# A block of attention, pooling and 64 experts on one core: a small expert group second, the p product in the routing stage, the shared expert once and late

## The chip, the core and the metric

The kernel runs on one core of a Trainium2 chip. Its time is the device time in microseconds, median of the runs. A core has five engines with a queue of instructions each: PE (matrix products, with weight loads beside them), DVE (vectors), ACT (scalar functions, also a cheap way out of PSUM), POOL (which here issues the gathers and scatters of rows) and SP (which issues most other transfers). Sixteen DMA engines move the data. The engines wait for each other by semaphores.

## The reference

One layer on x of 512 tokens by 1024, all in float32:

```
h = rmsnorm(x)
x = x + (sigmoid(g_a) * pool_branch(h) + sigmoid(g_b) * attention_branch(h)) @ w_out
h2 = rmsnorm(x)
scores = sigmoid(h2 @ w_router)                    # 64 experts, 8 chosen for each token
x = x + swiglu(h2, shared expert) + sum over the chosen experts of weight * swiglu(h2, expert)
x = x + sigmoid(rmsnorm(x) @ w_ple_gate) * rmsnorm(p @ w_ple_proj, g_ple_post)
```

An expert has three matrices of 1 MB: gate and up (1024 x 256 each) and down (256 x 1024). The shared expert has the same shapes and works on every token. p is 512 x 256, w_ple_proj 256 x 1024 (1 MB).

## The kernel before

Each engine has its program, written out by hand in the order of time; nothing is scheduled by a planner.

**Start.** PE first multiplies a tile of zeros with itself (`WARMING` times, L1796), then transposes the first 128 rows of x (`strided_T`, L1785) and takes the first half of Q (`first_q`, L1809) with weights called q0. SP loads x, q0, q1 and so on in the order of use.

**Dense part**, to about 320 us: Q, K, V, pooling, gates, attention, the two branches, `out_proj` (L2026), the second norm and the router.

**Routing**, about 320 to 341 us. DVE picks 8 experts for each token, ranks the tokens of every expert, and sorts the experts by a key: experts 0 to 3 first, the others by their count. `perm` is the matrix that turns a rank into a place in this order. While PE waits for these steps it takes products that nobody waits for yet: in the kernel before, the gate and up products of the shared expert for the first two of the four tiles of 128 tokens (`shared_up`, L2097, eight products of 512 columns for a tile). The rows of h2 go to DRAM (`h_rows`), and POOL gathers from there the rows of each expert step (`gather`, L812) as soon as the list of the step is made.

**Expert stage**, about 341 to 904 us. The 64 experts in sorted order make 16 groups of four. A large group has 96 places for each expert, so 384 rows, three steps of 128; a small group has 64, so two steps (`cap_of`, `steps_of`). Before, groups 0 to 7 are large and 8 to 15 small: 40 steps. A step r on PE is `up(r)` (L2273, 64 products of 32 rows), transposes of the step before, `rows_T(r + 1)`, the lists of a later group (`lists`), late jobs, and `down(r - 1)` (L2302). The weights of four experts fit into the ring of twelve 1 MB slots (`EXPERT_SLOT`: slots 9, 0, 3, 6 and the two behind each; gate, up, down). SP refills a slot when PE has done with it: `load_in` waits for `gu_ps`, `load_down` for `y_ps`, all in one fixed order (`load_group`). The ring is full with the first four experts when the stage begins, apart from what the code loads late.

**Late jobs** are small pieces that PE does between the parts of a step, at the steps listed in `JOB_STEP`: the shared expert for the last two tiles (`late_T`, `late_up`, L2072, L2083, L2086), its transposes, its down product (`shared_down`, L2222, then `base` on DVE), and the product p x w_ple_proj (`ple_proj`, L2233, then `ple_square` on ACT and `ple_gain` on DVE). `SMALL_AT` is 24, the first step of group 8. The weights of the shared expert are loaded twice: into the ring for the first two tiles, and into other buffers for the last two.

**Tail**, from about 904 us: the scattered results are summed, the last norm, w_ple_gate and the output.

Of the kernel before, what the change touches and what calls it, by code (L numbers as in the profile page):

```python
# [14 lines left out]
P = 128  # L15
# [25 lines left out]
WARMING = 14  # L41
# [8 lines left out]
BIG_GROUPS = 8  # L50
CAP2 = 64
LESS = CAP - CAP2
STEP_OF = [(g, s) for g in range(NGROUP) for s in range(GROUP * (CAP if g < BIG_GROUPS else CAP2) // P)]
STEPS = len(STEP_OF)
FIRST_STEP = [STEP_OF.index((g, 0)) for g in range(NGROUP)]
TCOL, WCOL = 2, 4
LCOL = TCOL + 2 * WCOL
LATE = (2, 3)
SMALL_AT = GROUP * CAP * BIG_GROUPS // P
JOB_STEP = [SMALL_AT + n // 2 for n in range(8)] + [SMALL_AT + 6 + n // 2 for n in range(4 * NT)]  # L60
# [13 lines left out]
C_ALL = C_IC + NG * PAD  # L74
# [7 lines left out]
def cap_of(g):  # L82

    return CAP if g < BIG_GROUPS else CAP2
# [19 lines left out]
def constant_table():  # L104
# [14 lines left out]
    for g, at in ((0, C_PAIR), (BIG_GROUPS, C_PAIR2)):  # L119
        for step in range(steps_of(g)):  # L120
            for k in range(STRIPS):
                second = strip_expert(g, step, k) - pair_of(g, step)
                c[k * STRIP:(k + 1) * STRIP, at + 2 * step + second] = 1
    for g, w in enumerate(POOL_WINDOWS):
        c[:, C_IC + g * PAD:C_IC + (g + 1) * PAD] = 1.0 / np.minimum(np.arange(PAD) + 1, w)
# [8 lines left out]
def alibi_table():  # L134
# [18 lines left out]
    ["wa0", "wa1", "wb0", "wb1"] + [f"out{c}" for c in range(4)] + ["shg", "shu"]  # L153
DENSE_SLOT = [u % 8 for u in range(13)] + [8, 9, 10, 11] + [1, 2, 3, 4, 6, 7]
# [5 lines left out]
SH_BANK = [7, 3, 5, 5]  # L160
# [21 lines left out]
def build(nc, t, y_dram, h2_dram, out):  # L182
    ctx = ExitStack()
    with ctx:
# [49 lines left out]
        sh_row = hi[:, 0:NT * FE].rearrange("p (i f) -> p i f", i=NT)  # L234
        sh_act = hi[:, 2 * T:4 * T].rearrange("p (j n) -> p j n", j=2)
        w_shd = hi[:, 2 * D:4 * D].rearrange("p (j n) -> p j n", j=2)
# [4 lines left out]
        shg_late = hi[:, 2 * D:4 * D].rearrange("p (k n) -> p k n", k=KD)  # L241
        shu_late = [w.rearrange("p (k n) -> p k n", k=KD // 2) for w in (lo3, hi[:, D:2 * D])]
# [7 lines left out]
        pT = qa[:, 0:1024].rearrange("p (j n) -> p j n", j=2)  # L250
        r_sc, r_sel, r_w, r_rank = (qa[:, 1024 + k * NR:1024 + (k + 1) * NR] for k in range(4))
# [25 lines left out]
        w_ple = [rows[:, 3, :], flat_actT[:, 3 * D:4 * D]]  # L277
# [17 lines left out]
        def bank(b, n=1):  # L295
# [26 lines left out]
        mid_loaded, late_loaded, sh_late_loaded = sem("mid_loaded"), sem("late_loaded"), sem("sh_late_loaded")  # L322
# [5 lines left out]
            sem("ple_ps"), sem("ple_squared"), sem("ple_copied"), sem("ple_rstd"))  # L328
        logit_ps, scores_ready = sem("logit_ps"), sem("scores_ready")
# [34 lines left out]
        def unit_source(name):  # L364
# [13 lines left out]
            if name == "shg":  # L378
                return t["w_sh_gate"][0].rearrange("(k p) n -> p k n", p=P)
            if name == "shu":  # L380
                return t["w_sh_up"][0].rearrange("(k p) n -> p k n", p=P)
# [101 lines left out]
        def _(sp):  # L483

            released_by = {"q0": (qkv_ps, 2 * NT), "q1": (qkv_ps, 2 * NT), "kv": (qkv_ps, 2 * NT)}
            released_by |= {"pool0": (gate_ps, 14), "pool1": (gate_ps, 14)}
# [31 lines left out]
            for u in range(8, DENSE_AT["shg"]):  # L518
                load_dense(u)
# [4 lines left out]
            for u in range(DENSE_AT["shg"], N_DENSE):  # L524
                load_dense(u)
# [37 lines left out]

            load_in(0, 0)
            load_down(0, 0)
            load_part(1, 1, 0)
            load_down(2, 2)
            load_down(3, 3)
# [4 lines left out]
            load_in(2, 2)  # L573
            sp.wait_ge(logit_ps, NT)
            sp.wait_ge(pT_ps, 2)
            sp.wait_ge(sel_ready, NT)
            sp.wait_ge(gathered[0], 16)
            sp.dma_start(shg_late, unit_source("shg")).then_inc(sh_late_loaded, 16)
            for c in range(2):
                sp.dma_start(shu_late[c], unit_source("shu")[:, 4 * c:4 * c + 4, :]).then_inc(sh_late_loaded, 16)  # L580
            sp.dma_start(gpost, t["g_ple_post"].broadcast_to([P, D])).then_inc(late_loaded, 16)
            sp.wait_ge(shared_ps, 2)
            load_in(3, 3)
            sp.wait_ge(order_ready, 1)

            def load_ple_proj():
                sp.wait_ge(tokw_ready, 1)
                for j in range(2):
                    sp.dma_start(w_ple[j], t["w_ple_proj"][0][j * P:(j + 1) * P, :]).then_inc(late_loaded, 16)

            def load_shared_down():
                sp.wait_ge(shared_ps, NT)
                sp.dma_start(w_shd, t["w_sh_down"][0].rearrange("(j p) n -> p j n", p=P)).then_inc(late_loaded, 16)

            def load_group(g, late):
# [6 lines left out]
                if e:  # L602
                    in_used(step)
                    load_in(pos, e[0])
                    if g == 1:
                        load_ple_proj()
                    if g - 1 >= BIG_GROUPS:
# [5 lines left out]
                if e and g - 1 < BIG_GROUPS:  # L613
# [9 lines left out]
                elif e:  # L623
                    in_used(step + 1)
                    if step == SMALL_AT + 2:
# [263 lines left out]
        def _(act):  # L889
# [86 lines left out]
            second_rows(3)  # L976
            act.wait_ge(maskedT_ps, 1)
# [3 lines left out]
            def shared_silu_of(i):  # L981
                act.wait_ge(shared_ps, i + 1)
                nc.scalar.activation(sh_row[:, i, :], bank(SH_BANK[i])[:, 0:FE], ACT.Silu,
# [9 lines left out]
            def silu(r, k):  # L993
                act.wait_ge(gu_ps, STRIPS * (r + 1))
                nc.scalar.activation(esilu[k], bank(2 + k)[:, 0:FE], ACT.Silu).then_inc(silu_ready, 1)  # L995
# [1464 lines left out]
```

## Time and profile before

| | us |
|---|---|
| median of 3 runs | 985.17 (983.69 to 985.89) |
| profiled execution | 985.45 |
| its span, first to last instruction | 983.6 |
| PE busy | 937.1 |
| DVE, ACT, POOL busy | 361.7, 162.7, 226.5 |
| chain of work that ended last | PE 74%, DMA 21% of the span |

The span is what the trace covers; the 1.8 us between it and the time of the execution lie outside. A busy PE may still be behind its peak, and idle time on another engine costs nothing by itself. The chain of work goes back from the last instruction to what released it, step by step.

### The profile page before, as it was taken

How to read it: one execution, taken by the hardware profiler on the slowest of the kernel's cores; microseconds unless marked ns; L12 is line 12 of the kernel's file. 1: busy time of each engine (PE TensorE's matmuls, PEld its weight loads, DVE VectorE, ACT ScalarE, POOL GpSimd, SP SyncE). 2: the span in 40 equal slices, each digit the busy share in tenths (PEclk: the TensorE clock that was granted, in tenths of full speed). 3: DMA queues.
4: the chain of work that ended last, by engine and by line, in shares of the span. 5: the costliest groups of instructions: out<-in, count | busy, mean ns of one | idle time of the engine just before them, and what ended most of it. 6: DMA issues, size and time to landing. Idle time of an engine off the chain costs nothing.

```text
span 983.6 us, 15761 instructions
## 1 busy us (share of the span) xinstructions
PE 937.1 (95%) x6411; PEld 492.3 (50%) x6411; DVE 361.7 (37%) x776; ACT 162.7 (17%) x304; POOL 226.5 (23%) x344
## 2 busy tenths in 40 slices
PE   9999999999999999999999999999889899897798
PEld 8688888888556533333333333344323233332344
DVE  3765674336436733333332110111101111111687
ACT  2001234210011211111111111111101112121021
POOL 4216923262000212222222222212111211201110
PEclk9999999999999999999999999999989999999899
DMA  9940006322472799999999999999999999999972
GB/s 335 329 128 1 1 1 208 135 86 79 142 304 107 242 383 395 395 418 400 404 421 411 402 417 409 411 420 422 415 421 422 421 419 416 421 398 372 368 274 86
DMA packets 83913, 301.06 MB, mean 306 GB/s; under 512 B 9299, under 2 KB 35959, under 8 KB 59648
## 3 DMA queue, kind: packets, MB, share of 16 engines
q1 hardware_dynamic: 70144, 263.19, 68.0%
q0 software_dynamic: 11920, 33.63, 8.8%
q10 hardware_dynamic: 1776, 3.21, 0.9%
q8 instruction: 52, 0.85, 0.3%
q14 instruction: 21, 0.17, 0.1%
HBM read 279.26 MB, written 29.36 MB: 314 GB/s over the span
## 4 chain that ended last, share of the span: by engine, by line
PE 74%; DMA 21%; SPq 2%; DVE 2%; issue 1%; ACT 0%; ACTq 0%
PE ps L2273 22%; DMA ring<-in_w_exp_up 18%; PE ps L1876 12%; PE ps L2302 8%; PE ps L2026 6%; PE ps L2005 5%; PE ps L2417 4%; PE ps L1785 2%; PE ps L1818 2%; DMA ring<-in_w_exp_down 2%; PE ps L2097 1%; PE ps L1828 1%; DMA ring<-accumulator 1%; SPq L548 1%; PE ps L2282 1%; SPq L534 1%
## 5 line engine op out<-in xcount | busy, mean ns | idle before, releaser
L2273 PE MATMUL ps<-ring,gates 128*32 128x512 f32 x2560 | 287.0, 600 | 27.3 <-DMA ring<-in_w_exp_up 26.5
L2273 PEld LDWEIGHTS ps<-ring,gates 128*32 128x32 f32 x2560 | 88.2, 111 | 218.0 <-issue 217.1
L2302 PE MATMUL ps<-ring,poolbuf 128*32 128x512 f32 x1280 | 147.3, 601 | 3.0 <-DMA ring<-in_w_exp_down 2.1
L1599 DVE COPY poolbuf<-ps 128x256 f32<-128x256 f32 x40 | 17.0, 425 | 355.9 <-PE ps L2282 355.9
L800 POOL TENSOR_TENSOR tickets<-cst 128x1 f32<-128x1 f32 x77 | 14.6, 189 | 397.4 <-ACT actT L1003 392.0
L2302 PEld LDWEIGHTS ps<-ring,poolbuf 128*32 128x32 f32 x1280 | 38.3, 110 | 84.6 <-issue 83.0
L1003 ACT ACTIVATE actT<-ps,qT 128x1024 f32<-128x1024 f32 x40 | 44.6, 1114 | 143.9 <-PE ps L2302 143.9
L995 ACT ACTIVATE poolbuf<-ps 128x256 f32<-128x256 f32 x40 | 15.4, 384 | 278.8 <-PE ps L2273 278.8
L1876 PE MATMUL ps<-xrow,ring 128*128 128x256 f32 x256 | 57.9, 381 | 0.1
L2026 PE MATMUL ps<-ring,gates 128*128 128x512 f32 x128 | 56.4, 594 | 0.0
L1876 PEld LDWEIGHTS ps<-xrow,ring 128*128 128x128 f32 x256 | 48.3, 190 | 8.5 <-issue 1.7
L1876 PE MATMUL ps<-actT,ring 128*128 128x256 f32 x208 | 47.5, 381 | 0.0
L812 POOL DMA_INDIRECT rows<-h_rows,stage x40 | 41.8, 1046 | 21.4 <-issue 18.9
L1785 PE MATMUL ps<-cst,rows 128*128 128x128 f32 x352 | 46.1, 274 | 0.0
L817 POOL DMA_INDIRECT accumulator<-actT,stage x40 | 40.6, 1016 | 22.1 <-issue 22.1
L1785 PEld LDWEIGHTS ps<-cst,rows 128*128 128x128 f32 x352 | 43.1, 191 | 2.0 <-issue 1.8
L2417 PE MATMUL ps<-ring,actT 128*128 128x512 f32 (+1 forms) x112 | 42.2, 531 | 0.0
L1876 PEld LDWEIGHTS ps<-actT,ring 128*128 128x128 f32 x208 | 39.0, 190 | 6.3 <-issue 0.9
L750 POOL TENSOR_TENSOR ring<-ring 128x1024 f32<-128x1024 f32 x12 | 28.3, 2360 | 52.7 <-DMA ring<-in_w_gate 30.5
L2026 PEld LDWEIGHTS ps<-ring,gates 128*128 128x128 f32 x128 | 23.8, 190 | 26.8 <-issue 26.8
L2417 PEld LDWEIGHTS ps<-ring,actT 128*128 128x128 f32 x112 | 20.9, 190 | 18.0 <-issue 17.2
L2282 PEld LDWEIGHTS ps<-cst,poolbuf 128*128 128x128 f32 x80 | 12.6, 206 | 33.5 <-issue 33.5
(303 smaller groups left out, 1072.3 us busy)
## 6 DMA issues: line engine op xcount, KB each, us to landing
ring<-in_w_exp_down SPq DMA_DIRECT2D x64, 1024.0 KB, 17.4
ring<-in_w_exp_gate SPq DMA_DIRECT2D x62, 1024.0 KB, 13.3
ring<-in_w_exp_up SPq DMA_DIRECT2D x62, 1024.0 KB, 16.3
ring<-accumulator SPq DMA_DIRECT2D x12, 1024.0 KB, 13.2
ring<-in_w_gate SPq DMA_DIRECT2D x8, 1024.0 KB, 11.7
ring<-in_w_in SPq DMA_DIRECT2D x5, 1024.0 KB, 10.1
xrow<-in_x SPq DMA_DIRECT2D x8, 512.0 KB, 6.4
accumulator<-ring SPq DMA_DIRECT2D x1, 4096.0 KB, 19.5
```

The source lines that it names most:

```text
L750: nc.gpsimd.tensor_tensor(dst, a, b, ALU.subtract).then_inc(wsum_ready, 1)
L812: pool.indirect_dma_start(hg[j], None, h2_dram, bass.IndirectOffsetOnAxis(ap=stage[:, 0, j, :], axis=0), bounds_check=T - 1, oob_is_err=Fa ...
L817: pool.indirect_dma_start(y_dram, bass.IndirectOffsetOnAxis(ap=stage[:, 1, j, :], axis=0), yrow[j], None, bounds_check=ACC_ROWS - 1, oob_i ...
L1003: nc.scalar.activation(yrow[j], bank(6, 2), ACT.Copy, scale=slot_wr[:, r, 0:1]).then_inc(y_ready, 1)
L1785: last = nc.tensor.transpose(bank(b0 + half)[:, k * width:(k + 1) * width], v[0:width, 4 * half + k, :], ident[0:width, 0:width])
L1876: last = mm(out[:, f * HALF_T:(f + 1) * HALF_T], w[:, k, f * P:(f + 1) * P], x[:, k, :], start=(k == 0), stop=(k == 3))
L2005: last = mm(bank(2 + c % 4)[:, f * HALF_T:(f + 1) * HALF_T], w[:, k, (2 * p + f) * P:(2 * p + f + 1) * P], x[:, k, :], start=(k == 0), sto ...
L2026: last = mm(bank(half), gates[:, k, i * P:(i + 1) * P], w[:, k], start=(n == 0), stop=(n == KD - 1))
L2273: last = mm(bank(2 + k)[part, :], hgT[k][:, q, part], pair_view(EXPERT_SLOT[js[c]])[:, q], start=(q == 0), stop=(q == KD - 1))
L2282: last = nc.tensor.transpose(bank(4)[:, q * P:(q + 1) * P], v[:, q, :], ident)
L2302: last = mm(bank(6 + half)[part, :], eactT[r % 2][:, q, part], w[:, q, half * 512:(half + 1) * 512], start=(q == 0), stop=(q == 1))
L2417: last = mm(gate_bank(i, n0)[:, 0:width], xT, unit_view(s, 4)[:, k % 4, n0 % 512:n0 % 512 + width], start=(k == 0), stop=(k == KD - 1))
```

## The change

It does five things.

1. `WARMING` is 8 instead of 14.
2. Group 1 becomes a group of 64 places and group 8 one of 96 (`EARLY`, `LARGE`). The sorted places 4 to 7 take the experts of ranks 32 to 35 (`RANK_AT`, in `perm`), so the same experts as before have 64 places; only their turn moves. There are 40 steps again. The lists are made at the steps in `LIST_STEP`.
3. The product p x w_ple_proj moves into the routing stage, in the places of `shared_up`. w_ple_proj goes into ring slot 8 as unit "ple", the fourth expert's down slot, so that this expert's down weights are loaded after the product. ACT copies each half (128 x 512) out of PSUM and squares it into a junk buffer (`ple_evict`); the multiplication with the gain is a step on DVE at steps 16 to 23.
4. The shared expert is computed late for all four tiles. Its gate and up weights are loaded once, in four pieces of 512 KB, two of them before the routing is over.
5. The jobs (twelve for the four tiles, two transposes, eight halves of the down product) stand at steps 24 to 38.

```diff
-WARMING = 14
+WARMING = 8
...
+EARLY = 1
+LARGE = [g for g in range(BIG_GROUPS + 1) if g != EARLY]
...
+LIST_STEP = [0, 1, 2, 4, 7, 10, 13, 15] + [2 * BIG_GROUPS + n for n in range(NGROUP - BIG_GROUPS)]
...
-JOB_STEP = [SMALL_AT + n // 2 for n in range(8)] + [SMALL_AT + 6 + n // 2 for n in range(4 * NT)]
+RANK_AT = list(range(GROUP)) + list(range(GROUP * BIG_GROUPS, GROUP * BIG_GROUPS + GROUP)) + \
+    list(range(GROUP, GROUP * BIG_GROUPS)) + list(range(GROUP * BIG_GROUPS + GROUP, NE))
+JOB_STEP = [SMALL_AT + n for n in (0, 0, 1, 3, 4, 4, 5, 5, 6, 7, 8, 8, 9, 9)] + \
+    [SMALL_AT + 11 + n // 2 for n in range(2 * NT)]
+GAIN_AT = NGROUP
...
+            def load_shared(n):
+                w = t["w_sh_gate" if n < 2 else "w_sh_up"][0].rearrange("(k p) n -> p k n", p=P)
+                sp.dma_start(sh_late[n], w[:, 4 * (n % 2):4 * (n % 2) + 4, :]).then_inc(sh_late_loaded, 16)
...
-                if e and g - 1 < BIG_GROUPS:
+                if e and g - 1 in LARGE:
...
+            def ple_evict(n):
+                i, half = PLE_TILE[n // 2], n % 2
+                act.wait_ge(ple_ps, n + 1)
+                nc.scalar.activation(pp[:, i, half * 512:(half + 1) * 512], bank(PLE_BANK[n]), ACT.Copy
+                                     ).then_inc(ple_copied, 1)
+                if n >= 3:
+                    act.wait_ge(ple_squared, n - 2)
+                nc.scalar.activation(ple_junk[n % 3], bank(PLE_BANK[n]), ACT.Square,
+                                     accum_out=st[:, 2, 2 * i + half:2 * i + half + 1]).then_inc(ple_squared, 1)
...
-            nc.vector.tensor_scalar(perm, cst[0:NE, C_IOTA:C_IOTA + NE], pos_col, None, ALU.is_equal
+            nc.vector.tensor_scalar(perm, cst[0:NE, C_RANK:C_RANK + NE], pos_col, None, ALU.is_equal
...
+                if GAIN_AT <= r < GAIN_AT + 2 * NT:
+                    ple_gain(r - GAIN_AT)
...
-            shared_up(0, 1, 6)
+            ple_proj(1, 6)
...
-                if 1 <= r < NGROUP:
-                    lists(r)
+                if r in LIST_OF:
+                    lists(LIST_OF[r])
```

How the instructions stand on SP, from the loads after `out_proj` to the first refill of the ring: before,

```order
L534 DMA ring<-in_w_exp_gate 128x2048 [waits x1_ps]
L534 DMA ring<-in_w_exp_up 128x2048
L578 DMA gates<-in_w_sh_gate 128x8x256 [waits sel_ready,gathered0,pT_ps,logit_ps]
L580 DMA gates<-in_w_sh_up 128x4x256 x2
L581 DMA gates<-in_g_ple_post 128x1024
L534 DMA ring<-in_w_exp_gate 128x2048 [waits shared_ps]
L534 DMA ring<-in_w_exp_up 128x2048
```

and now (the line numbers are those of the changed file):

```order
L543 DMA ring<-in_w_exp_gate 128x2048 [waits x1_ps]
L543 DMA ring<-in_w_exp_up 128x2048
L590 DMA gates<-in_g_ple_post 128x1024
L577 DMA gates<-in_w_sh_gate 128x4x256
L577 DMA actT<-in_w_sh_gate 128x4x256 [waits logit_ps]
L562 DMA ring<-in_w_exp_down 128x2048 [waits ple_ps]
L577 DMA qT<-in_w_sh_up 128x4x256
```

The gain and half of the shared gate weights come ahead of the routing's end, and the fourth expert's gate and up weights have gone to an earlier place; its down weights stand here instead.

On PE, from the last piece of the routing to the first expert step: before,

```order
L2097 MATMUL ps<-ring,actT 128x512 x2
L1785 MATMUL ps<-cst,rows 128x128 [waits ssq2_done,gathered0]
L1785 MATMUL ps<-cst,rows 128x128 x7
L2097 MATMUL ps<-ring,actT 128x512 x4
L2273 MATMUL ps<-ring,gates 32x512 [waits slot_loaded10,slot_loaded0,slot_loaded9,slot_loaded1,hgT_hi_ready,hgT_lo_ready]
L2273 MATMUL ps<-ring,gates 32x512 x31
```

and now

```order
L2126 MATMUL ps<-ring,qT 128x512 [waits ple_squared]
L2126 MATMUL ps<-ring,qT 128x512
L1811 MATMUL ps<-cst,rows 128x128 [waits ple_squared,gathered0]
L1811 MATMUL ps<-cst,rows 128x128 x7
L2126 MATMUL ps<-ring,qT 128x512 [waits ple_squared]
L2126 MATMUL ps<-ring,qT 128x512 x3
L2290 MATMUL ps<-ring,gates 32x512 [waits slot_loaded10,slot_loaded0,slot_loaded9,slot_loaded1,hgT_hi_ready,hgT_lo_ready]
L2290 MATMUL ps<-ring,gates 32x512 x31
```

The p products (L2126) stand where the shared products (L2097) stood, as many of them, with waits for ACT's squares (`ple_squared`) that free a PSUM bank.

## Rows read from the trace of the kernel before

**Rows 1.** The waits of PE, longest in total: us in all, times, longest us.
```profile
PE ps L2273 <- DMA ring<-in_w_exp_up: 26.5, 14, 5.6
```

**Rows 2.** Expert stage by windows; last columns are clock, DMA share, GB/s.
```profile
347.80:369.70 21.90, 21.17 (x221) 8.90 (x218) 6.52 (x24) 3.25 (x6) 4.47 (x10) 1.00 0.98 377
369.70:541.20 171.50, 171.50 (x1762) 67.17 (x1762) 57.53 (x213) 29.55 (x43) 39.64 (x84) 1.00 1.00 407
541.20:631.00 89.80, 87.13 (x784) 31.63 (x786) 10.55 (x24) 15.92 (x23) 19.81 (x42) 1.00 1.01 409
631.00:870.00 239.00, 217.30 (x1636) 87.21 (x1628) 34.32 (x65) 35.57 (x59) 39.78 (x85) 0.98 1.01 419
```

**Rows 3.** Window of one large group early in the stage; columns as above.
```profile
399.50:436.50 37.00, 37.00 (x398) 14.65 (x390) 13.06 (x45) 6.29 (x9) 8.48 (x18) 1.00 1.00 404
```

**Rows 4.** Timeline of the start: start us, us, engine, line, operation, count.
```profile
1.04 6.34 PE L1796 MATMUL ps<-kT 128*128 128x128 f32 x28 [1.04 <-DVE kT L1114]
1.16 1.36 SPq L499 DMA_DIRECT2D ring<-in_w_in  x2
4.75 1.06 ACT L893 ACTIVATE rows<-xrow 128x1024 f32<-128x1024 f32 x1 [2.30 <-DMA xrow<-in_x]
7.18 1.08 PE L1785 MATMUL ps<-cst,xrow 128*128 128x128 f32 x8
9.20 3.72 PE L1809 MATMUL ps<-ring,actT 128*128 128x256 f32 x16 [0.94 <-DVE actT L1108]
```

**Rows 5.** DMA issue at 1.16 us (q0): median us from issue to landing.
```profile
ring<-in_w_in SPq DMA_DIRECT2D x1, 1024.0 KB, 6.6
```

**Rows 6.** PE's timeline in the routing stage.
```profile
322.17 4.51 PE L2097 MATMUL ps<-ring,actT 128*128 128x512 f32 x10
336.34 1.05 PE L1785 MATMUL ps<-cst,rows 128*128 128x128 f32 x8
340.76 7.07 PE L2273 MATMUL ps<-ring,gates 128*32 128x512 f32 x64
```

**Rows 7.** ACT: 512 columns (mean ns of one); its timeline at 330 us.
```profile
L1010 ACT ACTIVATE gates<-ps 128x512 f32<-128x512 f32 x8 | 4.8, 597 | 7.3 <-PE ps L2233 7.3
...
330.48 0.59 ACT L978 ACTIVATE gates<-ps 64x512 f32<-64x512 f32 x1 [6.70 <-PE ps L2175]
```

**Rows 8.** The first gather of rows: its issue, and the write that it follows.
```profile
323.81 0.33 ACTq L957 DMA_DIRECT2D h_rows<-rows  x1
...
330.30 1.19 POOL L812 DMA_INDIRECT rows<-h_rows,stage  x1 [0.87 <-POOL stage L805]
```

**Rows 9.** The first gather alone, and all 40, issue to landing.
```profile
rows<-h_rows,stage POOLq DMA_INDIRECT x1, 4.7
...
rows<-h_rows,stage POOLq DMA_INDIRECT x40, 10.3
```

**Rows 10.** DMA in two stretches of 4 us.
```profile
328.00:332.00 4.00, 4.00 (x30) 2.33 (x29) 2.34 (x15) 1.50 (x3) 1.60 (x3) 1.00 0.01 2
368.00:372.00 4.00, 4.00 (x58) 2.33 (x54) 1.97 (x8) 0.98 (x2) 0.04 (x1) 1.00 0.89 310
```

**Rows 11.** SP's issue at 369.65 us, its landing, all such loads.
```profile
369.65 0.33 SPq L534 DMA_DIRECT2D ring<-in_w_exp_gate  x1
...
ring<-in_w_exp_gate SPq DMA_DIRECT2D x1, 1024.0 KB, 6.1
...
ring<-in_w_exp_gate SPq DMA_DIRECT2D x62, 1024.0 KB, 13.3
```

**Rows 12.** PE's timeline at the last steps.
```profile
868.23 1.12 PE L2233 MATMUL ps<-rows,qT 128*128 128x512 f32 x2
869.19 1.02 PE L2233 MATMUL ps<-actT,qT 128*128 128x512 f32 x2
887.76 3.64 PE L2273 MATMUL ps<-ring,gates 128*32 128x512 f32 x32 [0.78 <-DMA ring<-in_w_exp_up]
893.90 5.34 PE L2302 MATMUL ps<-ring,poolbuf 128*32 128x512 f32 x32 [2.06 <-DMA ring<-in_w_exp_down]
```

More of the change, by code:

```diff
@@ L152 @@
 DENSE = ["q0", "q1", "kv", "pool0", "pool1"] + [f"gate{p + h * PAIRS}" for p in range(PAIRS) for h in range(2)] + \
-    ["wa0", "wa1", "wb0", "wb1"] + [f"out{c}" for c in range(4)] + ["shg", "shu"]
-DENSE_SLOT = [u % 8 for u in range(13)] + [8, 9, 10, 11] + [1, 2, 3, 4, 6, 7]
+    ["wa0", "wa1", "wb0", "wb1"] + [f"out{c}" for c in range(4)] + ["ple"]
+DENSE_SLOT = [u % 8 for u in range(13)] + [8, 9, 10, 11] + [1, 2, 3, 4] + [8]
 BRANCH_PHASES = 28
@@ L328, in build @@
             sem("ple_ps"), sem("ple_squared"), sem("ple_copied"), sem("ple_rstd"))
+        ple_junk = [poolbuf[:, E0 + k * 512:E0 + (k + 1) * 512] for k in range(3)]
         logit_ps, scores_ready = sem("logit_ps"), sem("scores_ready")
@@ L517, in _ @@
             sp.dma_start(y_rows[0], zero_row.unsqueeze(1).broadcast_to([P, TOPK, D])).then_inc(y_first, 16)
-            for u in range(8, DENSE_AT["shg"]):
+            for u in range(8, DENSE_AT["ple"]):
                 load_dense(u)
@@ L976, in _ @@
             second_rows(3)
+            def ple_evict(n):
[7 more added lines that the diff above has]
+                                     accum_out=st[:, 2, 2 * i + half:2 * i + half + 1]).then_inc(ple_squared, 1)
+            for n in range(3):
+                ple_evict(n)
             act.wait_ge(maskedT_ps, 1)
@@ L1023, in _ @@
             rows_hi(0, 0)
-            shared_silu_of(1)
+            for n in range(5, 2 * NT):
+                ple_evict(n)
             for r in range(STEPS):
@@ L2090, in shared_up, with late_up @@
-            def shared_up(i, k0, k1):
-                if i == 0 and k0 == 0:
-                    loaded("shg")
-                    loaded("shu")
-                w = pair_view(DENSE_SLOT[DENSE_AT["shg"]])
-                for k in range(k0, k1):
-                    last = mm(bank(SH_BANK[i]), actT[:, k, i * P:(i + 1) * P], w[:, k], start=(k == 0),
-                              stop=(k == KD - 1))
-                if k1 == KD:
-                    last.then_inc(shared_ps, 1)
+            def late_up(i):
+                pe.wait_ge(sh_late_loaded, 64)
+                pe.wait_ge(h2T_ready, 2 * NT + 2 * i + 2)
+                for up in range(2):
+                    for k in range(KD):
+                        last = mm(bank(5)[:, up * FE:(up + 1) * FE], xT_late[k // 4][:, k % 4, :],
+                                  sh_late[2 * up + k // 4][:, k % 4, :], start=(k == 0), stop=(k == KD - 1))
+                last.then_inc(shared_ps, 1)
@@ new lines, in ple_proj @@
+            def ple_proj(m0, m1):
+                for m in range(m0, m1):
+                    n, j = m // 2, m % 2
+                    i, half = PLE_TILE[n // 2], n % 2
+                    if m == 0:
+                        loaded("ple")
+                        pe.wait_ge(pT_ready, 2)
+                    if m == 2:
+                        pe.wait_ge(h2T_ready, 2 * NT)
+                    if m == 4:
+                        pe.wait_ge(ssq2_done, NT)
+                    if j == 0 and n in (4, 5, 6):
+                        pe.wait_ge(ple_squared, (1, 2, 5)[n - 4])
+                    last = mm(bank(PLE_BANK[n]), pT[:, j, i * P:(i + 1) * P], w_ple[:, j, half * 512:(half + 1) * 512],
+                              start=(j == 0), stop=(j == 1))
+                    if j == 1:
+                        last.then_inc(ple_ps, 1)
@@ L2221, in shared_down @@
                 for j in range(2):
[L2222 removed]
+                    last = mm(bank(5), sh_act[:, j, i * P:(i + 1) * P], w_shd[j][:, half * 512:(half + 1) * 512],
                               start=(j == 0), stop=(j == 1))
                 last.then_inc(shdown_ps, 1)
[L2226 to L2235 removed]
             def rows_T(r):
```

218 lines of the change are left out of this document (94 added, 124 removed).

## The prediction

> **What bounds the kernel now.** I read the waits of PE first, then the busy windows, then the timelines at the start, at the routing stage and at the last steps. PE seems to set the time, since it is busy for 937 of 983.6 us. But in the expert stage (340.8 to about 904 us) it has 26.5 us of waits, nearly all for weights of the next experts [rows 1]. The windows show why: from 347.8 to 870 us the share of the DMA engines is 0.98 to 1.01 [rows 2]. The ring of twelve 1 MB slots is full when the stage begins, so PE runs ahead at first and meets the queue later. The stage therefore ends when its bytes have been moved, and a byte taken away counts only where the queue would otherwise have had something behind it. Ahead of 340.8 us it is the other way round: PE goes from one product to the next through the routing [rows 6], while DMA moves 2 GB/s from 328 to 332 us [rows 10].
>
> **The change part by part.**
>
> *Six zero products fewer.* Fourteen take 6.34 us as 28 records of 226 ns; the eight transposes behind them, of the same size, take 1.08 us [rows 4], so the zero products ran at the lower of the two clocks. Eight would end near 1.04 + 8 x 0.453 = 4.7 us, when the first rows of x are there (ACT stops waiting for them at 4.75) [rows 4]. The 2.7 us are not all gained: the first Q product needs q0, which lands at 1.16 + 6.6 = 7.8 us [rows 4, 5], and starts at 9.20 now. So the gain is at most 1.4 us. On the other side, PE then has 3.6 us of unbroken work instead of 6.1, a short gap, the transposes and another gap of about a microsecond, and the clock may still be low when Q begins. That product is 16 records in 3.46 us now (the next row begins at 12.66); at half the clock it takes 6.9, ends at 14.7 and is 2.0 us late. Bounds: 1.4 gained, 2.0 lost. I take 0.3 lost, the middle, since the trace shows neither a shorter warm-up nor a gap in it.
>
> *The products that fill the routing.* Two shared tiles (16 products of 512 columns) leave, and the p product (8 halves of two, again 16 products of 512 columns) comes in the same places, as the order lists above show. At 4.51 us for five products [rows 6] that is 0.9 us each, out and in: no difference. What is new is that ACT empties each half at once: a copy of 597 ns [rows 7], a square of about the same and a read of the sum, some 1.4 us, eight times. ACT has room: it idles 6.7 us ahead of 330.48 [rows 7]. Five of the eight halves come before the copies that the first expert step waits for. Each costs 1.4 us if that room were gone; I take nothing.
>
> *Bytes out of the expert stage.* From 335 us on, the kernel before loads 6,656 KB beside the regular weights: gate and up of the shared expert a second time (2,048), the last gain (512), the fourth expert's gate and up (2,048), the p weights (1,024), the shared down weights (1,024). The kernel after loads 3,072 there: the fourth expert's down weights, half of the shared up and gate weights (1,024), the shared down weights. So 3,584 KB, 3.67 MB, move to stretches where DMA has little to do. At the 407 GB/s of the large groups [rows 2] that is 9.0 us of queue.
>
> I do not count them. The first group's slots are freed by PE's steps alone, one or two experts at a time, and the trace shows the queue run dry before its third step has freed the last: from 368 to 372 us the share is 0.89 and the rate 310 GB/s [rows 10], and a load issued at 369.65 lands after 6.1 us, little over half of its median of 13.3 [rows 11] and no more than q0 at the start of the program [rows 5]. All of the 3,584 KB lie before this point, and everything after it, the shared down weights too, is the same in both kernels. The saved 9 us thus become idle DMA between 341 and 370 us, and PE, which sets the pace there, does not arrive sooner. Zero, with 9.0 us as the bound if the queue kept its backlog.
>
> *The early group of 64 places.* The set of small experts is the same, and so are the 40 steps and the bytes; only one group of two steps moves from ninth to second place. PE then frees eight slots within two steps, and the queue has work from 382 us on. What this can bring is the difference between the rate while PE sets the pace, 404 GB/s in a large group [rows 3], and the rate when DMA does, 409 in the last large groups (541 to 631 us), where PE already waits [rows 2]. Over the 67 us to 436.5: 67 x (1 - 404/409) = 0.8 us. The upper bound takes the 419 of the small groups [rows 2] for the whole of 369.7 to 541.2: 171.5 x (1 - 407/419) = 4.9 us. I take 0.8, since large groups free their slots in the same rigid order after the change. Below, zero.
>
> *Jobs moved.* Four shared tiles instead of two, and no p products, in steps 24 to 38. Their columns are equal, and PE's waits there (most of the 26.5 us) cover both. The lists are made at other steps; their number and cost stay. The gain multiplication on DVE goes to steps 16 to 23, where DVE is busy for 57.5 of 171.5 us in the large groups [rows 2]: nothing. One thing is new at the end: step 38 has two halves of the shared down product, up to 1.98 us each [rows 12], and had none. Their cover is the waits that follow, 0.78 and 2.06 us [rows 12], which leaves 1.1 us; but the down product behind these waits took 5.34 us against 3.64 for another of 32 [rows 12], and may get back 1.7 if PE no longer idles before it. I take nothing, between 0.6 gained and 1.1 lost.
>
> *Sum.* 0.3 - 0.8 = 0.5 us less. The profiled execution took 985.45 us (a span of 983.6 and 1.8 around it), so 984.9; it is 0.3 above the median of the runs, which gives 984.6.
>
> **A rule that speaks against the change.** The trace has the low clock over the zero products and the high one right behind them [rows 4]. The Trainium skill, "TensorE: Matmul & The Clock Gate", Part 1, says that the low clock is the resting state and that sustained work releases it, so that a warm-up cut short is paid for by the products behind it. By that rule the start would cost the 2.0 us of the lower bound, and the forecast would be 986.3; by the row for the landing of q0 alone it would gain 1.4.
>
> **The rivals.**
> 1. *The clock is still low at the first Q product.* For it: the gaps named above. Against it: eight products and eight transposes are 5 us of work, not far from what was enough. 984.6 - 0.3 + 2.0 = 986.3 us.
> 2. *With the early group the queue always has a backlog* and runs at 419 GB/s. For it: the dips come at the ends of large groups. Against: 409 in the groups for which PE already waits. 4.9 instead of 0.8, so 980.5; with the start's gain 978.8.
> 3. *The saved bytes count.* For it: the share is near 1 from 342 us on. Against: rows 10 and 11. Half of 9.0 and more: 975 to 980.
> 4. *Slower: the first gather comes late.* The gain and half of the shared gate weights (1,536 KB, 4 us) now stand in the queue from 320 us, ahead of the write of the last rows (issued at 323.81) and of the gather that follows it (330.30) [rows 8]. That gather lands after 4.7 us [rows 9], at 335.0, and PE needs it at 336.34 [rows 6], so 1.3 us are spare. With a loaded queue the median is 10.3 [rows 9]: 5.6 more, 4.3 of them on PE's path, 988.9. For it: nothing else fills PE behind that gather. Against: DMA stands still from 328 to 332 us [rows 10], which is about where the added 4 us would end. It decides once the added loads run past 331.5 us.
>
> **How the numbers follow.** Forecast, no change worth the name: 0.36. Rival 1: 0.14. Rival 2: 0.20. Rival 3: 0.12. Rival 4: 0.18. A measurement of this kernel can tell about 0.2%, 2 us, from no change: faster means under 983.2, slower over 987.1. Rivals 2 and 3 are faster, and 0.02 of the forecast; the forecast and most of rival 1 are the same (0.46); rival 4 and 0.02 of rival 1 are slower. The range leaves out the far half of rival 3 and the far part of rivals 2 and 4: 978 to 988.5; the forecast's own is 982.5 to 987.
>
> **What would show it.** In the profile after, the first Q product's start and the length of its 16 records give the first term. The rate of DMA from 342 to 370 us should be lower than now, and the load issued after the second step's product should again land in about 6 us; if it takes over 9, rival 3 holds. PE's first wait for weights should come near step 5 instead of beyond 541 us, without the later windows of large groups going much over 409 GB/s. PE should go from the p products to the first row transposes without a wait; a wait for the gather there makes rival 4. I am wrong altogether if PE waits less than about 20 us in the expert stage, since then it, and not the queue, sets the end.

## The result, and the profile after

The changed kernel takes 988.61 us (median of 22 runs, 985.11 to 991.33) against 986.91 us before (22 runs, 983.69 to 988.70): a ratio of 1.0022, 95% interval 1.0013 to 1.0032, so 1.3 to 3.2 us slower. The forecast was 0.6 us faster. The before of these 22 runs lies 1.7 us above the median of three runs to which the forecast's sum was tied; it is the ratio that is to be explained. The profiled execution took 987.73 us (span 985.9).

The waits of PE in the changed kernel (us in all, times, longest):

```profile
PE ps L2290 <- DMA ring<-in_w_exp_up: 26.2, 10, 8.4
PE ps L2415 <- DVE xrow L1763: 9.2, 4, 5.6
...
PE ps L1811 <- DMA rows<-h_rows,stage: 0.3, 1, 0.3
```

The wait for weights is as long as before [rows 1], in fewer and longer pieces, and there is a new, short one for the first gather. Now the windows of the expert stage, for rows 2 (the last is cut at 650 and 700 us; behind each window stand its length and PE's busy time, and at the end PE's granted clock, the DMA share and GB/s):

```profile
347.80:369.70 21.90, 21.17 (x213) 8.90 (x212) 7.06 (x26) 3.14 (x6) 4.48 (x10) 1.00 0.86 317
369.70:541.20 171.50, 163.26 (x1541) 61.79 (x1543) 35.55 (x110) 27.84 (x40) 36.90 (x78) 0.97 1.00 409
541.20:631.00 89.80, 87.58 (x886) 33.91 (x882) 33.52 (x116) 14.68 (x22) 19.87 (x42) 1.00 1.00 400
631.00:650.00 19.00, 19.00 (x187) 6.72 (x180) 4.01 (x18) 3.21 (x5) 5.68 (x12) 1.00 1.01 409
650.00:700.00 50.00, 50.00 (x420) 22.11 (x423) 7.94 (x16) 8.86 (x13) 8.70 (x19) 1.00 0.97 382
700.00:870.00 170.00, 154.62 (x1188) 67.22 (x1184) 23.16 (x45) 21.27 (x32) 28.18 (x59) 0.96 1.01 420
```

and the kernel before in one window that the rows above did not show:

```profile
650.00:700.00 50.00, 50.00 (x389) 25.48 (x382) 7.74 (x15) 7.24 (x11) 6.47 (x14) 1.00 1.01 418
```

Read PE's busy time and the last three columns. At 347.8 us the rate has fallen from 377 to 317 GB/s, lower as forecast. From 369.7 to 541.2 PE now waits (163.26 of 171.5 us busy, against all of it), and DMA moves 2 GB/s more. The next window is lower (400 against 409); e3 below moves still less there, 395, and loses nothing by it. What matters comes later: from 650 to 700 us PE is busy throughout, as before, but DMA moves 382 GB/s against 418. That is 50 us x 36 GB/s = 1.8 MB left over, 4.3 us at the 420 GB/s of the next window. PE's timeline shows what it does there:

```profile
655.69 7.08 PE L2290 MATMUL ps<-ring,gates 128*32 128x512 f32 x64
...
663.92 1.89 PE L2107 MATMUL ps<-gates,mixw 128*128 128x256 f32 x8
665.65 1.89 PE L2107 MATMUL ps<-actT,qT 128*128 128x256 f32 x8
667.38 1.89 PE L2107 MATMUL ps<-qT,mixw 128*128 128x256 f32 x8
669.10 1.89 PE L2107 MATMUL ps<-rows,qT 128*128 128x256 f32 x8
...
674.38 7.05 PE L2290 MATMUL ps<-ring,gates 128*32 128x512 f32 x64
```

These are the up products of steps 25 and 26, and between them the gate and up product of the first shared tile (`late_up`, L2107). The steps are 18.7 us apart instead of 11.8, and no wait for weights stands ahead of either. Steps 24 and 25 were small-group steps before; with a small group moved to second place they are the last two of the last large group.

The start and the routing stage, for rows 4, 6 and 8:

```profile
1.04 3.79 PE L1822 MATMUL ps<-kT 128*128 128x128 f32 x16 [1.04 <-DVE kT L1132]
4.84 1.84 PE L1811 MATMUL ps<-cst,xrow 128*128 128x128 f32 x8
8.03 3.71 PE L1835 MATMUL ps<-ring,actT 128*128 128x256 f32 x16 [1.34 <-DVE actT L1126]
...
322.67 0.33 ACTq L967 DMA_DIRECT2D h_rows<-rows  x1
331.14 1.19 POOL L822 DMA_INDIRECT rows<-h_rows,stage  x1 [0.87 <-POOL stage L815]
335.73 1.16 PE L1811 MATMUL ps<-cst,rows 128*128 128x128 f32 x8 [0.35 <-DMA rows<-h_rows,stage]
340.26 7.07 PE L2290 MATMUL ps<-ring,gates 128*32 128x512 f32 x64
```

The first Q product starts 1.17 us earlier and takes 3.71 us, as long as before, so here the start gained 1.2 us. The write of the last rows is issued 1.14 us earlier, but the gather behind it 0.84 us later, and at the first up product 0.5 us is left. For rows 11, the load behind the second step's product:

```profile
368.95 0.33 SPq L543 DMA_DIRECT2D ring<-in_w_exp_gate  x1
...
ring<-in_w_exp_gate SPq DMA_DIRECT2D x1, 1024.0 KB, 7.0
```

The last steps:

```profile
890.10 7.07 PE L2290 MATMUL ps<-ring,gates 128*32 128x512 f32 x64
898.36 3.64 PE L2318 MATMUL ps<-ring,poolbuf 128*32 128x512 f32 x32 [0.75 <-DVE poolbuf L1623]
```

Where the kernel before waited for weights [rows 12], PE waits here only 0.75 us, for DVE: PE is late at the end, and not the queue.

### The profile page after: what moved, and what is told of

It is laid out like the page before. It is cut to its first block, busy times and chain, and to the rows that moved or that the text cites. A ratio compares the mean times of both kernels' runs of the same rounds, so it can differ in the third digit from the quotient of the medians.

```text
span 985.9 us, 15851 instructions
## 1 busy us (share of the span) xinstructions
PE 938.7 (95%) x6447; PEld 497.3 (50%) x6447; DVE 365.4 (37%) x784; ACT 166.2 (17%) x312; POOL 226.7 (23%) x344
## 4 chain that ended last, share of the span: by engine, by line
PE 75%; DMA 19%; DVE 2%; SPq 2%; issue 1%; ACT 1%; POOL 0%; ACTq 0%; POOLq 0%; DVEq 0%
PE ps L2290 24%; DMA ring<-in_w_exp_up 16%; PE ps L1902 12%; PE ps L2318 9%; PE ps L2052 6%; PE ps L2031 5%; PE ps L2431 4%; PE ps L1811 3%; PE ps L1844 2%; PE ps L2107 1%; PE ps L1854 1%; PE ps L2299 1%; DMA ring<-accumulator 1%; SPq L482 1%; DMA h_rows<-rows 1%
## 5 line engine op out<-in xcount | busy, mean ns | idle before, releaser
L2290 PE MATMUL ps<-ring,gates 128*32 128x512 f32 x2560 | 291.4, 608 | 26.9 <-DMA ring<-in_w_exp_up 26.2
```

Source lines behind the costliest of these rows:

```text
L2290: last = mm(bank(2 + k)[part, :], hgT[k][:, q, part], pair_view(EXPERT_SLOT[js[c]])[:, q], start=(q == 0), stop=(q == KD - 1))
```

## The experiments

My theory: the shared tile's product in steps 24 and 25 holds PE up where PE sets the pace, slots come free late, DMA goes idle, and the stretches behind it don't give that back. Rivals: the lists in steps 16 to 23; the start; the early group itself, with its long waits and the products at half clock behind them; the work in step 38; the late gather. "Up" is the start of the first up product in the profiled execution, "down" the end of its last down product, us. Each ratio is to runs of the kernel before made beside it, whose median was 986.97 for e1 to e4, 986.21 for e5 to e8 and 986.12 for e9 to e12; so kernels of different groups are compared by the ratios. There are 12 runs of each, 7 of e1 and 5 of e7.

| kernel | median | ratio to before (95%) | up | down |
|---|---|---|---|---|
| before | 986.91 | | 340.76 | 904.25 |
| after | 988.61 | 1.0022 (1.0013 to 1.0032) | 340.26 | 907.01 |
| e1 lists in steps 1 to 15 | 987.91 | 1.0035 (1.0020 to 1.0051) | 340.17 | 906.16 |
| e2 before, 8 zero products | 986.83 | 1.0005 (0.9989 to 1.0020) | 341.02 | 905.36 |
| e3 shared tiles from step 26 | 986.41 | 1.0003 (0.9989 to 1.0016) | 340.03 | 905.43 |
| e4 group in ninth place | 987.49 | 1.0022 (1.0007 to 1.0036) | 340.12 | 905.50 |
| e5 e3, none in step 38 | 986.17 | 1.0000 (0.9988 to 1.0012) | 340.93 | 904.34 |
| e6 e5, group in ninth place | 988.76 | 1.0026 (1.0010 to 1.0042) | 342.21 | 905.72 |
| e7 two tiles in large groups | 996.95 | 1.0106 (1.0090 to 1.0123) | 342.61 | 915.98 |
| e8 e5, loads behind the gather | 986.97 | 1.0014 (1.0000 to 1.0029) | 342.87 | 905.54 |
| e9 e5, 11 zero products | 986.21 | 1.0001 (0.9988 to 1.0015) | 340.37 | 904.56 |
| e10 e6, 11 zero products | 986.83 | 1.0005 (0.9994 to 1.0017) | 340.77 | 903.61 |
| e11 e8, 11 zero products | 986.69 | 1.0009 (0.9995 to 1.0023) | 339.41 | 905.61 |
| e12 before, 11 zero products | 985.52 | 0.9996 (0.9984 to 1.0008) | 339.51 | 904.99 |

**e1, the lists alone.**

```diff
-LIST_STEP = [0, 1, 2, 4, 7, 10, 13, 15] + [2 * BIG_GROUPS + n for n in range(NGROUP - BIG_GROUPS)]
+LIST_STEP = list(range(NGROUP))
```

> The changed kernel with the fifteen lists made one per step in steps 1 to 15, as before, instead of seven of them there and eight in steps 16 to 23. Nothing else moves. Theory A (the lists in steps 16 to 23 hold PE up just where PE has become the pace again, eight times 0.37 us, while the same lists in steps 1 to 15 would lie beside waits for weights): the steps of 558 to 656 us go from 12.13 to 11.76 us, and the time falls by 2 to 3 us, to 985.6 to 986.6. Theory B (the time is lost elsewhere: by the products at half clock behind long waits, by the work in step 38, or by the late gather): the steps get shorter there all the same, but PE waits as much longer in the small groups, and the time stays within 0.8 us of the changed kernel.

Theory B: 0.7 us below the changed kernel by the medians, and 1.0035 against 1.0022 by the ratios. The up product of step 22 came 2.4 us earlier (616.16 against 618.54), but the window of the shared tile took that back:

```profile
631.00:650.00 19.00, 19.00 (x175) 7.62 (x168) 2.96 (x7) 2.61 (x5) 4.72 (x11) 1.00 1.01 417
650.00:700.00 50.00, 50.00 (x421) 21.23 (x423) 6.93 (x14) 8.34 (x12) 9.72 (x21) 1.00 0.95 373
```

409 became 417 GB/s, then 382 became 373. The lists are not the cause.

**e2, the start alone.** Edit of the kernel before: `WARMING = 14` to `WARMING = 8`.

> The kernel before with eight zero products instead of fourteen, and nothing else changed. If the start is worth what the two traces show in the dense part, the first Q product begins at 8.0 us instead of 9.2 and every row up to the routing is 1.1 to 1.2 us earlier. Theory A (the expert stage of the kernel before is bound by the queue, so a start of PE that is earlier by 1.2 us also starts the loads of the experts earlier, and the whole 1.2 us is kept): 985.7 us against 986.9. Theory B (the bytes are what bounds it and their start does not move): the 1.2 us come back as waits for weights, and the time is within 0.4 us of the kernel before.

Theory B: no gain. In this execution the first Q product started at 7.80 us after a wait of 1.77 us and took 5.38 us instead of 3.7: the granted clock fell within it. This is taken up at e9.

**e3, the shared tiles' work out of steps 24 and 25.**

```diff
-JOB_STEP = [SMALL_AT + n for n in (0, 0, 1, 3, 4, 4, 5, 5, 6, 7, 8, 8, 9, 9)] + \
+JOB_STEP = [SMALL_AT + n for n in (2, 2, 3, 3, 4, 4, 5, 5, 6, 6, 7, 7, 8, 8)] + \
```

> The changed kernel with the shared tiles' work in steps 26 to 31 and their transposes of the activations in step 32, so that none of it lies in steps 24 and 25, the last two of the last large group; the work of steps 35 to 38 stays. Theory A (a product of 6.9 us with its transposes in steps 24 and 25 delays PE where no weight is waited for): 0.5 to 1.5 us faster than the changed kernel, 987.1 to 988.1. Theory B (the small groups' queue is full from 698 us on, so that what PE does earlier only lengthens its waits): within 0.4 us of 988.6.

Theory A, and 2.2 us by the medians (1.9 by the ratios, with intervals of 0.1 to 0.15% to either side) rather than 0.5 to 1.5: the whole loss against the kernel before is gone. The edit also spaces the later tiles differently, but all of those lie in small groups. The window now:

```profile
650.00:700.00 50.00, 46.98 (x374) 20.94 (x378) 6.42 (x13) 7.36 (x11) 8.48 (x18) 0.97 1.01 416
```

PE waits again (46.98 of 50 us busy) and DMA is back at 416 GB/s. The early group and its waits, the lists, the start and the loads ahead of the gather are as in the changed kernel, so the loss is not theirs. Of the window's 1.8 MB not all is lost in the end: from 700 to 870 us e3 moves 417 GB/s and the changed kernel 420, 0.5 MB the other way. This profiled execution took 988.03 us, 1.6 above e3's median, so its last column in the table says little.

**e4, the group back in ninth place**, with e1's lists:

```diff
-EARLY = 1
+EARLY = 8
-RANK_AT = list(range(GROUP)) + list(range(GROUP * BIG_GROUPS, GROUP * BIG_GROUPS + GROUP)) + \
-    list(range(GROUP, GROUP * BIG_GROUPS)) + list(range(GROUP * BIG_GROUPS + GROUP, NE))
+RANK_AT = list(range(NE))
```

> The changed kernel with the 64-place group put back to ninth place, and so with the lists in steps 1 to 15; the shared weights loaded once, the p products in the routing, the work in steps 24 to 38 and the eight zero products stay. Theory A (the early group makes PE wait early, with two up products at half the clock, and PE is the pace later with no queue to catch up from): 985.5 to 986.5 us, below the changed kernel by 2 to 3 us, with the first wait for weights beyond 541 us as before. Theory B (the early group brings the 0.8 us that were forecast, or nothing, and the loss is in the moved work of steps 24 to 38 or in the gather): 988.6 to 989.4 us.

Between the two by the median, 1.0 us above A's range and 1.1 below B's; by the ratio, 1.0022, it is as slow as the changed kernel, as B has it, though the shared tiles now lie in small groups. If the shared tile in the large group costs 2 us, then the early group would seem to have brought something that is lost here; e6 and e10 come back to that. But then something else in the change would cost about as much, since e4 has neither the tile in a large group nor the early group and is still 0.07 to 0.36% slower than before.

**e5, e3 with nothing in step 38.**

```diff
-    [SMALL_AT + 11 + n // 2 for n in range(2 * NT)]
+    [SMALL_AT + 10 + n // 2 for n in range(2 * NT)]
...
                     in_used(step)
+                    if step == SMALL_AT + 8:
+                        load_shared_down()
                     load_in(pos, e[0])
...
                     in_used(step + 1)
-                    if step == SMALL_AT + 8:
-                        load_shared_down()
```

> The kernel of e3 with the eight halves of the shared down product one step earlier, in steps 34 to 37, so that none lies in step 38; their weights are asked for one step earlier too. Theory A (at the end PE, not the queue, is late: the last up product starts at 888.5 to 890.1 us without a wait for weights, where it waited in the kernel before, and the two halves of step 38 of up to 1.98 us each stand on that path): the last up product starts 1 to 2 us earlier relative to the one before it, and the time is 0.5 to 1.5 us below e3, 985.0 to 985.9. Theory B (the last weights come no earlier, so the halves only take the place of a wait): within 0.4 us of e3, 986.0 to 986.8, with waits for weights before the last up or down products again.

Theory B by the time (0.2 us below e3 by the medians, 0.3 by the ratios). The last steps look as in the kernel before, down to the product at the lower clock behind the wait:

```profile
887.85 3.64 PE L2290 MATMUL ps<-ring,gates 128*32 128x512 f32 x32 [0.83 <-DMA ring<-in_w_exp_up]
893.98 5.34 PE L2318 MATMUL ps<-ring,poolbuf 128*32 128x512 f32 x32 [2.05 <-DMA ring<-in_w_exp_down]
```

The granted clock was 0.50 from 895 to 897 us, in the 5.34 us product. So the halves of step 38 had taken the place of these waits.

**e6, e5 with e4's edit and e1's lists.**

> The kernel of e5 with the 64-place group back in ninth place and the lists in steps 1 to 15: what is left of the change is the shared weights once, the p products in the routing, the later work and the eight zero products. It gives the worth of the early group alone, with the later work where the queue covers it. Theory A (the queue is busy nearly all the time from 370 us on with the group in either place: 2.9 us of idle DMA from 370 to 700 us in e3, 2.7 in e4): within 0.6 us of e5, and the rate from 370 to 541 us is 404 to 410 GB/s in both. Theory B (the early group keeps a backlog that brings the 0.8 us of the forecast, or the 4.9 of its bound): 0.8 to 4.9 us slower than e5.

2.6 us above e5, as theory B has it, but the profiled execution began its expert stage 1.3 us later for the clock at the start, and took 563.5 us for it, e5 563.4. The rates of the two differ where theory A had them equal. With the early group (e5), and with the group in ninth place (e6):

```profile
369.70:541.20 171.50, 163.97 (x1571) 62.87 (x1573) 38.02 (x114) 28.43 (x42) 36.74 (x78) 0.99 1.01 417
541.20:631.00 89.80, 87.26 (x870) 33.85 (x866) 31.57 (x112) 14.88 (x22) 19.78 (x42) 0.98 0.98 389
...
369.70:541.20 171.50, 171.50 (x1764) 66.88 (x1760) 57.31 (x212) 29.35 (x42) 39.73 (x84) 1.00 1.00 405
541.20:631.00 89.80, 86.49 (x780) 31.93 (x776) 15.60 (x32) 15.65 (x23) 19.86 (x42) 1.00 1.00 404
```

It is so in all traces: to 541 us the eight kernels with the early group move 408 to 417 GB/s and the six with the group in ninth place 404 to 407, but from 541 to 631 us it is 389 to 408 against 400 to 411. The early group brings bytes forward, and the groups behind it give part of that back.

**e7, the suspected cost doubled**, in e1:

```diff
-JOB_STEP = [SMALL_AT + n for n in (0, 0, 1, 3, 4, 4, 5, 5, 6, 7, 8, 8, 9, 9)] + \
+JOB_STEP = [SMALL_AT + n for n in (-3, -3, -2, -2, -1, -1, 5, 5, 6, 7, 8, 8, 9, 9)] + \
-GAIN_AT = NGROUP
+GAIN_AT = NGROUP - 4
```

> The suspected cost doubled: the kernel of e1 (lists in steps 1 to 15) with two shared tiles, transposes and products, in steps 21 to 23, inside the large groups, in place of the one tile in steps 24 and 25; the other two tiles stay in the small groups, and the gain multiplication comes four steps earlier. Theory A (work of 8 us that PE is given in the large groups delays the freeing of slots, the DMA engines run dry, and nothing later gives that back): 3 to 7 us slower than e1, 991 to 995 us, with 4 to 9 us of idle DMA between 560 and 700 us, against 3.6 in e1 (2.9 of it from 650 to 700). Theory B (the small groups' waits take all of it back): within 0.8 us of e1, 987.2 to 988.9.

Theory A, and at or above the top of its range: 9.0 us over e1 by the medians (996.95 against 987.91), 7.0 by the ratios. The windows:

```profile
631.00:650.00 19.00, 19.00 (x158) 7.83 (x157) 3.20 (x6) 3.25 (x5) 2.83 (x6) 1.00 0.87 334
650.00:700.00 50.00, 50.00 (x426) 21.13 (x428) 5.52 (x13) 7.68 (x13) 11.36 (x24) 1.00 0.85 332
700.00:870.00 170.00, 146.67 (x1122) 59.51 (x1118) 20.33 (x40) 21.43 (x31) 28.36 (x60) 0.93 1.01 421
```

Against e1 they move 19 x 83 + 50 x 41 GB/s = 3.6 MB less from 631 to 700 us, which at 421 GB/s is 8.6 us, and the time is 7 to 9 us longer. The second tile, 6.9 us of products and 1.3 of transposes, costs about its whole length; the first cost about 2.2 (e3). Why the first cost less is not shown; the tiles of e7 also stand three steps earlier. PE waits more than ever after 700 us (146.67 of 170 busy), and the time is no better for it, since the queue is full there (421 GB/s).

**e8, the loads behind the gather**, in e5, with e1's lists:

```diff
+            sp.wait_ge(gathered[0], 16)
             sp.dma_start(gpost, t["g_ple_post"].broadcast_to([P, D])).then_inc(gpost_loaded, 16)
             load_shared(0)
-            sp.wait_ge(logit_ps, NT)
             load_shared(1)
```

> The kernel of e5 with the loads of the gain and of half of the shared gate weights behind the first gather, so that they stand in front of neither the write of the last rows nor the gather, and with the lists in steps 1 to 15. Theory A (PE's start of the expert stage sets when slots come free, and so when everything later moves): the write of the last rows lands some 3.3 us after its issue as before, PE does not wait for the gather, the first up product starts 0.4 to 0.7 us earlier, at 339.5 to 339.7 us, and the time is 0.4 to 0.8 us below e5. Theory B (1.5 MB more in the queue at 335 us takes the place of the wait, or the lists cost as much where they now are): within 0.3 us of e5.

0.8 us above e5 by the medians, so theory A fails, but the profiled execution doesn't show why, since its first Q product took 3 us longer:

```profile
8.29 6.74 PE L1835 MATMUL ps<-ring,actT 128*128 128x256 f32 x16 [1.93 <-DMA ring<-in_w_in]
```

**e9 to e12, eleven zero products** in e5, e6, e8 and the kernel before: `WARMING = 11`.

> The kernel of e5 with eleven zero products. In nine executions with eight of them PE waited 1.05 to 2.29 us ahead of the first Q product, and in the four with the longest waits (1.77 to 2.29) the granted clock fell to its lower level within that product, which then took 5.38 to 6.74 us instead of 3.7. Eleven products end at 6.0 us and the transposes behind them at 7.1, so the first Q product starts at 8.1 to 8.6 us after a wait of about 1 us. Theory A (it is the wait that the clock answers to): 16 records in 3.7 us, and 0.5 to 1 us less than e5 in the mean, 985.2 to 986.0. Theory B (the length of the work ahead decides, or the start is worth nothing): the clock falls here too, or the time is that of e5, 986.2, within 0.4.

> The kernel of e6 (64-place group in ninth place) with eleven zero products; beside e9 it gives the worth of the early group without the scatter of the start. Theory A (the early group is worth nothing: from the first up product to the end of the last down product the profiled executions of e5 and e6 took 563.3 and 563.4 us): within 0.7 us of e9. Theory B (it is worth what the medians of e5 and e6, 986.2 and 988.8, say): 2 us or more slower than e9.

> The kernel of e8 (gain and half of the gate weights behind the first gather, lists in steps 1 to 15) with eleven zero products. From the first up product to the end of the last down product the profiled execution of e8 took 562.6 us, the shortest of ten, but it began 2.6 us later than the changed kernel, since its first Q product took 6.74 us. Theory A (with the clock high at the start that length stays): the first up product at 340.0 to 340.6 us, the last down product's end at about 903, and 984.5 to 985.5 us, below e9. Theory B (the loads behind the gather bring nothing): within 0.5 us of e9.

> The kernel before with eleven zero products, nothing else. Theory A (the start's gain is kept when the clock stays high): the first Q product at 8.1 to 8.6 us instead of 9.20, the first up product as much earlier, and 985.4 to 986.0 us, 0.6 to 1.0 below the kernel before. Theory B (the queue takes it back in the expert stage): within 0.4 us of the kernel before.

The start first. With eight zero products the clock was low in the first Q product in four of nine profiled executions: it fell within the product in three, and in e8 it was low from its start (0.50 from 8 to 9 us), which the expectation of e9 has as a fall within it. Here are its granted levels in e6, where PE had waited 2.29 us (0.50 is 1.2 GHz, 1.00 is 2.4):

```profile
8.00:10.00 2.00, 1.60 (x4) 1.33 (x5) 0.39 (x1) 0.00 (x0) 0.00 (x0) 0.65 1.11 360
10.00:12.00 2.00, 2.00 (x6) 1.59 (x5) 0.00 (x0) 0.00 (x0) 0.00 (x0) 0.50 1.04 380
12.00:14.00 2.00, 2.00 (x12) 1.79 (x12) 0.00 (x0) 1.15 (x2) 0.14 (x1) 1.00 1.10 352
```

The product then took 5.38, 5.38, 5.38 and 6.74 us, after waits of 1.77, 2.29, 2.09 and 1.93 us; in the other five it took 3.7 after waits of 1.05 to 1.73. With eleven it took 3.7 in all four, after waits up to this one in e9:

```profile
8.13 3.72 PE L1835 MATMUL ps<-ring,actT 128*128 128x256 f32 x16 [1.83 <-DVE actT L1126]
```

So the clock stayed high as theory A of e9 has it, though not by the wait alone: 1.83 us stayed high here, 1.77 fell with eight. Four executions are few: where five of nine stay high, four in a row would come about one time in ten. In the times theory B holds for e9, which is as fast as e5, and for e11, 0.5 us above e9 by the medians. For e12 it is open: 0.4 us gained by the ratio is B, 0.6 by the medians is A, and the interval is 1.2 us to either side. Its first up product starts 1.25 us earlier than before, but its last down product ends 0.74 later. In e11 the gather came at 328.96 and PE did not wait for it:

```profile
328.96 1.19 POOL L822 DMA_INDIRECT rows<-h_rows,stage  x1 [0.87 <-POOL stage L815]
...
335.00 1.04 PE L1811 MATMUL ps<-cst,rows 128*128 128x128 f32 x8
...
339.41 7.07 PE L2290 MATMUL ps<-ring,gates 128*32 128x512 f32 x64
```

Its last down product nevertheless ends at 905.61. Over all kernels without a shared tile in a large group, the first up product starts between 339.41 and 342.87 us and the last down product ends between 903.61 and 905.72, and neither follows the other: a start that is up to 3.5 us later is not seen at the end, as if the queue took the difference back. e10 is 0.6 us above e9 by the medians, which is theory A, and 0.4 by the ratios.

## Why the prediction was wrong

**The step that failed** is "Jobs moved": "PE's waits there (most of the 26.5 us) cover both", at a cost of nothing. The waits of before lie in the small groups, all but 2.1 us from step 24 on. With one small group moved from ninth to second place, steps 24 and 25 belong to the last large group, where PE has no wait (631 to 700 us), and the change leaves the first shared tile there. The prediction used the step numbers with the cover that they had before the move, though it named the move in the paragraph before. e3 gives this term 2.2 us (1.9 by the ratios), and e7 shows the mechanism with a second dose. It is as large as the whole loss against before, 1.7 by the medians and 2.2 by the ratio. The columns are not equal either, as that paragraph has them: the two more late tiles bring transposes of 1.3 us each.

**The start**, 0.3 lost with bounds of 1.4 gained and 2.0 lost: the middle lies within the interval of e2 (1.1 us gained to 2.0 lost), and single executions came near both bounds (1.3 gained in e1, 2.1 lost in e8). Rival 1 happened in four of nine profiled executions, at 1.7 us in three of them and 3.0 in one, beside a start that was otherwise 0.6 to 1.4 us earlier. The sum has the first Q product end at 12.66 us; the next row begins at 12.76, so it takes 3.56 us and the lower bound is 2.2. What the start gains or loses is not seen at the end of the expert stage. The Trainium skill, "TensorE: Matmul & The Clock Gate", Part 1, has the low clock as the default, which activity releases; as the prediction used it (a warm-up cut short is paid for by the products behind it), it agrees with these four traces (5.38 to 6.74 us for the product), and not with the five others (3.7). The same part of the Trainium skill says that the number of slow products at a kernel's start varies from run to run, so the two outcomes do not speak against it.

**Bytes out of the expert stage**, nothing: right as far as the traces go. The 317 GB/s at 347.8 to 369.7 us, at a DMA share of 0.86 against 0.98, show part of the saved bytes as idle DMA (21.9 us x 60 GB/s = 1.3 of 3.67 MB), and a load issued at 368.95, behind the second step's product, landed after 7.0 us. Rival 3 did not occur: e4, e6 and e10, which keep the saved bytes without the early group, are no faster than before. No run changes the bytes alone.

**The early group**, 0.8 gained with a bound of 4.9: the sign is likely right, the size not settled. Three pairs differ in the group's place, e4 and e3, e6 and e5, e10 and e9; by their ratios the ninth place is slower by 1.9, 2.6 and 0.4 us, each uncertain by about 2 (two intervals of 0.12 to 0.16% to either side). (In the first pair the later jobs stand at other steps too, all in small groups.) PE waits from step 4 on, a step earlier than forecast. Rival 2's 419 GB/s did not come, but its direction is there: 408 to 417 from 369.7 to 541.2 us with the early group, 404 to 407 without. What the prediction did not have is the lower rate behind it. By the means of these windows over all traces (412.3 against 405.5 GB/s, then 399.1 against 406.7) it is some 2.8 us of queue gained and 1.6 given back at 420 GB/s, an estimate. The long waits and the products at half clock behind them did not show as a loss: e3 has the early group too (PE is busy for 161.4 of the 171.5 us to 541.2) and is as fast as before.

**The gather**, rival 4: its mechanism is there and its size was wrong. PE waits 0.35 us for it instead of 4.3, and e11, without the wait, is no faster than e9. (The 1,536 KB of this rival are the gain and all of the shared gate weights, not half of them.)

**The fill of the routing and the end**, nothing each: right. From 320 to 347.8 us PE is idle for 0.35 us, the wait for the gather, so the p products run in place without one of their own; and e5 against e3 puts the work of step 38 at 0.2 to 0.3 us, within the noise.

**The test that was to show me wrong** did not: PE's waits are 26.2 us, as long as before. A total hides where they lie. The same sum stood beside a time 2 us longer, with the waits at other steps.

Still open: how much the early group brings; what else the change costs; and whether any of these versions beats the kernel before. The three kernels with the group in ninth place and no tile in a large group (e4, e6, e10) are 2.2, 2.6 and 0.5 us slower than before, each uncertain by 1.1 to 1.6. So it seems that the rest of the change costs a microsecond or two, which the early group repays in e3 and e5; no run shows where. None of the versions beats the kernel before by these runs; the nearest is e12, at 0.9996.

## What to carry to other kernels

Work that is hidden behind a wait is hidden behind the wait of one place: when a change reorders the places, look up again, step by step, which work now stands where the waiting is. Where a full transfer queue sets the time, a stretch in which compute alone sets the pace is lost queue time that later waits don't give back in full (e7: 7 to 9 us for 8.2 us of work), so extra work belongs in the steps that wait. Do not count a faster start or saved bytes against such a queue before a run shows their worth: here starts of the stage that differed by up to 3.5 us ended within 2.1 us of each other, in another order, and no kernel with fewer bytes was faster.

## What the runs showed of the hardware

The granted clock fell from 1.00 to 0.50, behind eight zero products and eight transposes, in some executions and not in others, with the same instructions of PE ahead of it and nearly the same wait (1.72 and 1.73 us without a fall in e1 and e5, 1.77 with one in e2). And the executions of most kernels scatter by 4 to 7.6 us (983.55 to 989.29 in 30 runs of the kernel before), so that 12 runs of a kernel still left intervals of 0.23 to 0.32% of the time from end to end, and a single profiled execution says little about a difference of 2 us.
